# Applying the second model's first norm factor to the products' results

## The chip, the cores and the metric

The kernel runs on one NeuronCore of a Trainium2 chip (trn2). The metric is the time of one execution on the device in microseconds (us); lower is better. The core has five engines that run their own instruction streams in order and meet at semaphores: TensorE (PE in the rows, its weight load PEld), VectorE (DVE), ScalarE (ACT), GpSimd (POOL), and SyncE (SP), which here only issues transfers. All arithmetic is float32; a float32 matrix product is made of three float32r products.

## The reference

Two models run one after the other on 256 tokens of 1024 features. The first ends in a feed-forward layer and a layer norm, the second begins with an RMS norm and one wide input product. Cut to what lies on both sides of the boundary:

```python
x = layer_norm(ALPHA * x + swiglu_ffn(x, ffn_w_in[i], ffn_w_down[i]), ln_ffn_g[i], ln_ffn_b[i])
...
h = rmsnorm(x, ln1[l])                    # x * rsqrt(mean(x * x) + 1e-6) * g
z = h @ w_in[l]
ml_qk, ml_v, ml_o, ml_i, ml_f, fx_q, fx_k, fx_v, fx_f = jnp.split(z, splits, axis=-1)
ml_qk = jax.nn.silu(causal_conv(ml_qk, ml_conv_w[l], ml_conv_b[l]))
...
x = x + cross_attention(rmsnorm(x, ln_x[l]), rmsnorm(mem, ln_mem[l]), w_xq[l], w_xkv[l], w_xo[l])
```

ml_i, ml_f and fx_f are the gates (16 columns); the mLSTM takes ml_qk, ml_v, ml_o, the forgetting attention fx_q, fx_k, fx_v.

## The kernel before

Tokens lie in two tiles of 128 rows (TT = 2), features in eight tiles of 128 (KT = 8). `x_tm` holds the residual token-major, `x_hi` and `x_lo` the normalized rows feature-major, split into a float32r high part and the rest. All big weights come as 164 slabs of 128x2048, streamed in order by SyncE through three raw buffers. For each slab ScalarE makes `w_hi` (line 602), VectorE `w_lo = w_raw - w_hi` (line 1364), each in a ring of three (WS = 3), and TensorE forms hi x hi, lo x hi and hi x lo (lines 2087 to 2089). `after(i)` on ScalarE and VectorE is the split of slab i + 3; ScalarE's waits until TensorE is done with slab i, VectorE's until ScalarE is, and SyncE's load of slab i + 3 until VectorE is done with slab i. The order on each engine is written out by hand.

The input product of the second model takes 14 slabs: ml_qk 4, ml_v 2, ml_o 2, fx_qk 4, fx_v 2. ml_qk and fx_qk come out feature-major (features on partitions), ml_v, ml_o and fx_v token-major. Each goes to one of three PSUM banks and ScalarE takes it from there (`take`, line 1061); TensorE's slab n waits for take n - 3. Behind the first ml_qk slab TensorE does the gate product (`gates`, 24 matmuls).

Norms are numbered. Norm 3 is the first model's last layer norm, norm 4 the second model's first RMS norm, norm 5 that of `mem`. A usual layer norm (`norm`, lines 981 and 1683, used for norms 0 to 2) takes statistics on VectorE, the root on ScalarE, writes normalized rows to `xn`, and lets TensorE transpose them (`transposes`, line 2490), with `warm` matmuls of the identity (line 2158) between; gain and offset are applied per feature behind the transposes, and POOL makes x_tm from xn with `gain_offset` (lines 1328 and 1329), spread over the next feed-forward layer. Norms 3 and 4 together are `last_of_first_model` (lines 1000 and 1713): VectorE applies norm 3's gain and offset to x_tm by rows, ScalarE squares the rows (line 913), takes the roots, and only then are the rows of norm 4 normalized and transposed.

After that ScalarE starts the transfer of `mem` into `gain` (line 1142); VectorE makes the gates' logarithms, running sums and maxima (lines 1905 to 1913) with ScalarE's Exp and Ln between, then four w_lo, the memory norm, and the convolution over ml_qk (lines 1928 and 1936). POOL has nothing to do in the second model.

Of the kernel before, what the change touches and what calls it, by code (L numbers as in the profile page):

```python
# [157 lines left out]
def build(nc, d, out, upto=99):  # L158
# [4 lines left out]
    with ExitStack() as ctx:  # L163
# [107 lines left out]
        gsel = sb("gsel", [P, 12, P], F32R, a_m)  # L271
        sel = sb("sel", [P, 12], where=a_m)
# [21 lines left out]
        with ExitStack() as a:  # L294
# [15 lines left out]
            se_o = sb("se_o", [P, 2, T], where=a)  # L310
            ml_y = x_fm[:, 0:4, :].rearrange("p a (b c) -> p (a b) c", c=P)
# [144 lines left out]
        rstd_ready, xn0_ready, xn_act, xn_dve = sem("rstd_ready"), sem("xn0_ready"), sem("xn_act"), sem("xn_dve")  # L456
        zero_set, half_hi = sem("zero_set"), sem("half_hi")
# [9 lines left out]
        STATS_BEFORE = {0: 0, 1: 2, 2: 4, 3: 6, 4: 8, 8: 11}  # L467
# [118 lines left out]
        def _(act):  # L586
# [354 lines left out]
            def to_features(q, k):  # L941
# [39 lines left out]
            def norm(q, second=None):  # L981

                if NORMS[q][4]:
                    for t in range(TT):
                        deviation(q, t)
                        normalized(q, t, x_tm)
                        if t == 0:
                            hi_half(second, 0)
                else:
# [10 lines left out]
            def last_of_first_model():  # L1000
# [145 lines left out]

            def takes(section, n, dst, scale=lambda j: 1.0):
                for j in range(n):
                    take(P_FIRST[section] + j, first[section] + j, dst(j), scale(j))
            takes("ml_qk", 4, lambda j: conv_in[:, 2 * j:2 * j + 2, 3:T + 3])  # L1150
# [3 lines left out]
            act.wait_ge(mem_loaded, 16)  # L1154
            for t in range(TT):
                squares_of_all(5, t, gain)
            normalized(5, 1, gain)
            takes("ml_v", 2, lambda j: ml_v[:, :, 256 * j:256 * j + 256])
# [5 lines left out]
            for j in range(2):  # L1164
                act.wait_ge(slab_done, first["ml_o"] + j + 1)
                n = P_FIRST["ml_o"] + j
                nc.scalar.activation(ml_o[:, :, 256 * j:256 * j + 256], ps[:, n % 3, :].rearrange("p (a b) -> p a b", a=2),
                                     ACT.Sigmoid).then_inc(p_taken, 1)
                after(first["ml_o"] + j)
# [4 lines left out]
            dst = lambda j: fx_v[:, :, 256 * j:256 * j + 256]  # L1174
            take(P_FIRST["fx_v"], first["fx_v"], dst(0))
# [4 lines left out]
            take(P_FIRST["fx_v"] + 1, first["fx_v"] + 1, dst(1))  # L1180
# [83 lines left out]
        def _(pool):  # L1264
# [68 lines left out]
            for q in range(3):  # L1333
                pool.wait_ge(xlo_ready, KT * FM_NORMS.index(q) + KT)
                pool.wait_ge(gain_loaded, 32 * (q + 1))
                for t in range(TT):
                    for n in range(2):
# [4 lines left out]
                        gain_offset(q, t, n)  # L1342


        @block.vector
        def _(dve):
# [274 lines left out]
            def scales(q, t):  # L1621
# [3 lines left out]
                if NORMS[q][4] and q != 3:  # L1625
# [14 lines left out]
            def to_features(q, k):  # L1640

                name, g_at, b_at, e, mean = NORMS[q]
                dve.wait_ge(tr_ready, KT * FM_NORMS.index(q) + 2 * (k // 2) + 2)
                if b_at:
# [38 lines left out]
            def norm(q, scale, last_slab, product):  # L1683
# [9 lines left out]
                features(q)  # L1693
# [18 lines left out]

            def last_of_first_model(scale, last_slab, product):

                def centred(t, at):
                    return V.scalar_tensor_tensor(x_tm[:, t, at], x_tm[:, t, at], mv[:, t, 0:1], gain[:, 0, at],
                                                  ALU.subtract, ALU.mult)

                def scaled(t, at):
                    dve.wait_ge(rstd_ready, 6 + t + 1)  # L1720
                    V.scalar_tensor_tensor(x_tm[:, t, at], x_tm[:, t, at], rstd[:, t:t + 1], gain[:, 1, at],
                                           ALU.mult, ALU.add).then_inc(stat_ready, 1)

                first_half_sums(scale, last_slab, product)
                dve.wait_ge(gain_loaded, 128)
                link(centred(0, slice(0, C)))
                scales(3, 0)
                link(add_product(x_tm, scale, 1, 1, last_slab, product))
                link(half_statistics(1, 1))
                mean_variance(1)  # L1730
                scaled(0, slice(0, C))
                scales(3, 1)
                link(centred(1, slice(0, 512)))
                scaled(1, slice(0, 512))
                link(centred(1, slice(512, C)))
# [150 lines left out]
            for i in (2, 3):  # L1886
                after(first["moba_o"] + i)
# [1009 lines left out]
```

## Time and profile before

| | us |
|---|---|
| median of 3 runs (1186.64 to 1189.3) | 1189.04 |
| the profiled execution | 1189.56 |
| its span, first to last instruction | 1187.8 |
| TensorE busy | 1147.4 |
| VectorE busy | 746.9 |
| ScalarE busy | 621.1 |
| POOL busy | 109.9 |

All rows of this document are of one profiled execution; their times count from the span's start. Engines overlap, so busy times don't add up. The chain that ended last is the sequence of instructions that released one another up to the end; its shares say where a saved microsecond would count. A duration includes the time that an instruction waits for a port after its issue. TensorE's matmuls are pipelined: a record is longer than the distance to the next one, and the distance is what counts. The mean granted clock of TensorE was 0.997 of full speed.

### The profile page before, as it was taken

The numbers are of one execution on the slowest core, as the hardware profiler recorded it, in microseconds if no ns is written. First come the engines' busy times: TensorE is split into PE (matmuls) and PEld (weight loads), VectorE is DVE, ScalarE is ACT, GpSimd is POOL, SyncE is SP. The second block draws the span as 40 slices with busy tenths as digits, with TensorE's granted clock in tenths as the row PEclk, the third lists the DMA queues.
The fourth block names the chain that finished last, engine by engine and source line by source line (L and its number), as shares of the span: only waits on it lengthen the run. The fifth ranks groups of instructions, "written<-read, shape, count | busy, mean of one in ns | idle before, by whom it ended". The sixth has DMA issues, their size and how long they took to land.

```text
span 1187.8 us, 24912 instructions
## 1 busy us (share of the span) xinstructions
PE 1147.4 (97%) x10626; PEld 1046.4 (88%) x10626; DVE 746.9 (63%) x1081; ACT 621.1 (52%) x906; POOL 109.9 (9%) x87
## 2 busy tenths in 40 slices
PE   6999989999999999999999999999998999999997
PEld 6798777789999989987999999899997898999996
DVE  7888776475544467896655444768486555655554
ACT  8974553354344345664733433665565564544443
POOL 0032263601100000220010000000000000000000
PEclk9999999999999999999999999999999999999999
DMA  8531111046545644433555446354533442655550
GB/s 302 217 106 50 50 49 49 25 156 231 190 167 188 246 179 156 165 109 141 178 213 182 179 172 248 107 211 177 179 118 131 143 176 92 239 180 181 212 177 36
DMA packets 29805, 187.32 MB, mean 158 GB/s; under 512 B 3472, under 2 KB 5648, under 8 KB 8592
## 3 DMA queue, kind: packets, MB, share of 16 engines
q1 hardware_dynamic: 27072, 177.21, 41.4%
q10 hardware_dynamic: 2640, 8.75, 2.3%
q8 instruction: 73, 1.20, 0.4%
q14 instruction: 20, 0.16, 0.0%
HBM read 184.90 MB, written 1.05 MB: 157 GB/s over the span
## 4 chain that ended last, share of the span: by engine, by line
PE 82%; DVE 10%; ACT 4%; issue 2%; DMA 0%; POOL 0%; ACTq 0%; DVEq 0%; SPq 0%
PE ps L2087 24%; PE ps L2088 23%; PE ps L2089 23%; DVE w_lo L1364 1%; PE ps L2411 1%; PE ps L2416 1%; PE ps L2557 1%; PE ps L2220 1%; ACT mixed L631 1%; DVE w_lo L1360 1%; PE ps L2413 1%; PE ps L2304 1%; PE ps L2353 1%; PE ps L2799 1%; PE ps L2807 1%
## 5 line engine op out<-in xcount | busy, mean ns | idle before, releaser
L1364 DVE TENSOR_TENSOR w_lo<-w_raw,w_hi 128x2048 fp32r<-128x2048 f32 x149 | 346.0, 2339 | 133.2 <-ACT w_hi L602 132.8
L2087 PE MATMUL ps<-x_hi,w_hi 128*128 128x256 f32 x1344 | 378.2, 281 | 4.3 <-DVE x_lo L1651 2.4
L2088 PE MATMUL ps<-x_lo,w_hi 128*128 128x256 f32 x1344 | 374.9, 279 | 0.0
L2089 PE MATMUL ps<-x_hi,w_lo 128*128 128x256 f32 x1344 | 374.8, 279 | 0.0
L602 ACT CAST w_hi<-w_raw 128x2048 fp32r<-128x2048 f32 x148 | 281.7, 1906 | 150.2 <-PE ps L2089 149.1
L2087 PEld LDWEIGHTS ps<-x_hi,w_hi 128*128 128x128 f32 x1344 | 252.6, 188 | 10.7 <-issue 5.6
L2088 PEld LDWEIGHTS ps<-x_lo,w_hi 128*128 128x128 f32 x1344 | 252.7, 188 | 1.3
L2089 PEld LDWEIGHTS ps<-x_hi,w_lo 128*128 128x128 f32 x1344 | 252.7, 188 | 0.0
L2087 PE MATMUL ps<-w_hi,hid_hi 128*128 128x512 f32 x304 | 118.7, 391 | 0.1
L2088 PE MATMUL ps<-w_lo,hid_hi 128*128 128x512 f32 x304 | 118.7, 390 | 0.0
L2089 PE MATMUL ps<-w_hi,hid_lo 128*128 128x512 f32 x304 | 118.3, 389 | 0.0
L1779 DVE TENSOR_TENSOR hid<-act_f,ps 128x512 f32<-128x512 f32 x22 | 15.1, 688 | 127.0 <-PE ps L2089 127.0
L1033 ACT ACTIVATE act_f<-ps 128x512 f32<-128x512 f32 x38 | 22.7, 598 | 123.4 <-PE ps L2089 123.4
L2087 PE MATMUL ps<-w_hi,mix_hi 128*128 128x512 f32 (+1 forms) x192 | 73.0, 380 | 0.6 <-DVE mix_lo L1829 0.3
L2088 PE MATMUL ps<-w_lo,mix_hi 128*128 128x512 f32 (+1 forms) x192 | 68.1, 354 | 0.0
L2089 PE MATMUL ps<-w_hi,mix_lo 128*128 128x512 f32 (+1 forms) x192 | 68.0, 354 | 0.0
L2089 PEld LDWEIGHTS ps<-w_hi,hid_lo 128*128 128x128 f32 x304 | 57.1, 188 | 12.2
L2087 PEld LDWEIGHTS ps<-w_hi,hid_hi 128*128 128x128 f32 x304 | 57.1, 188 | 11.4 <-DVE hid_lo L1785 0.5
L2088 PEld LDWEIGHTS ps<-w_lo,hid_hi 128*128 128x128 f32 x304 | 57.1, 188 | 10.5
L2087 PE MATMUL ps<-w_hi,x_hi 128*128 128x256 f32 x224 | 63.0, 281 | 0.0
L2089 PE MATMUL ps<-w_hi,x_lo 128*128 128x256 f32 x224 | 62.9, 281 | 0.0
L2088 PE MATMUL ps<-w_lo,x_hi 128*128 128x256 f32 x224 | 62.9, 281 | 0.0
(399 smaller groups left out, 1779.0 us busy)
## 6 DMA issues: line engine op xcount, KB each, us to landing
w_raw<-in_weights SPq DMA_DIRECT2D x163, 1024.0 KB, 4.9
xt<-in_xT SPq DMA_DIRECT2D x2, 512.0 KB, 5.4
w_raw<-in_weights SPq DMA_DIRECT2D x2, 512.0 KB, 6.2
x_tm<-in_x SPq DMA_DIRECT2D x1, 1024.0 KB, 5.0
gain<-in_mix_g ACTq DMA_DIRECT2D x2, 512.0 KB, 3.7
gain<-in_mix_b ACTq DMA_DIRECT2D x2, 512.0 KB, 5.9
gain<-in_ffn_g ACTq DMA_DIRECT2D x2, 512.0 KB, 7.4
gain<-in_ffn_b ACTq DMA_DIRECT2D x2, 512.0 KB, 9.5
```

The lines of the kernel that those rows point to most:

```text
L602: nc.scalar.copy(w_hi[:, i % WS, :], w_raw[:, i % RAW, :]).then_inc(hi_done, 1)
L631: nc.scalar.activation(mixed[:, q % 2, k, :], xt[:, k, :], ACT.Copy, scale=less_mu[:, at:at + 1]).then_inc(scaled_ready, 1)
L1033: nc.scalar.activation(act_f[:, j % 2, :], ps[:, 4 + 2 * (j % 2), :], ACT.Relu if name == "ff2" else ACT.Silu).then_inc(ffn_act, 1)
L1360: ins = V.tensor_tensor(halves_placed(w_lo[:, i % WS, :], m), halves_first(w_raw[:, i % RAW, :], m), halves_placed(w_hi[:, i % WS, :], m). ...
L1364: V.tensor_tensor(w_lo[:, i % WS, :], w_raw[:, i % RAW, :], w_hi[:, i % WS, :].bitcast(F32), ALU.subtract).then_inc(lo_done, 1)
L1779: V.tensor_tensor(hid[:, j % 2, :], act_f[:, j % 2, :], ps[:, 5 + 2 * (j % 2), :], ALU.mult).then_inc(ffn_taken, 1)
L2087: nc.tensor.matmul(out, hi_l, hi_r, start=start, stop=False)
L2088: nc.tensor.matmul(out, hi_l, lo_r, start=False, stop=False)
L2089: return nc.tensor.matmul(out, lo_l, hi_r, start=False, stop=stop)
L2220: last = mm(both[q][:, T * m + c0:T * m + T], src[f, 2 * m + t, :], ar[f, 2 * g + m, t, :, :].rearrange("p s c -> p (s c)")[:, c0:T], star ...
L2304: last = mm(z[half, HD * h:HD * h + HD], dd[half, t, 0, s, :], u_m[half, HD * h:HD * h + HD], start=True, stop=True)
L2353: last = mm(ps[0:hi_c - lo_c, 5, at:at + T], g1[:, k, lo_c:hi_c], mixed[:, 1, k, :], start=k == 0, stop=k == KT - 1)
```

## The change

Norm 3 becomes a usual norm. Its normalized rows are transposed, and behind the transposes each feature is multiplied by norm 3's gain times norm 4's, plus norm 3's offset times norm 4's (two small tiles computed earlier). What remains of norm 4 is one factor per token, which commutes with the product. It is formed while the products run: POOL makes x_tm (8 instructions), ScalarE squares it, VectorE inverts the root (`factor_col`), spreads it over 128 columns (`factor_wide`), TensorE transposes it behind the third ml_qk slab, and VectorE copies it out (`factor_row`). Token-major results are scaled in ScalarE's take (one instruction per row tile in place of one), the gates by VectorE, feature-major ones by eight multiplies of POOL; the convolution waits for four of them, the mLSTM's scores for all. The gate chain moves behind this and behind the memory norm; `mem` goes to conv_out's space.

```diff
@@ ScalarE, features @@
+                if q == 4:
+                    return nc.scalar.activation(x_fm[:, k, :], feature_tile(q, k), ACT.Identity,
+                                                scale=ln1_gain[:, k:k + 1], bias=ln1_offset[:, k:k + 1])
@@ ScalarE @@
+            def squares_of_residual():
+                junk = x_fm[:, :, :].rearrange("p (t a) c -> p t (a c)", t=TT)
                 for t in range(TT):
-                    deviation(3, t)
-                act.wait_ge(stat_ready, STATS_BEFORE[4] + 1)
-                squares_of_all(4, 0, x_tm)
-                squares_of_half(4, 0)
-                normalized(4, 0, x_tm)
-                squares_of_half(4, 1)
-                normalized(4, 1, x_tm)
-                features(4)
+                    act.wait_ge(xtm_ready, 7 + t)
+                    link(nc.scalar.activation(junk[:, t], x_tm[:, t, :], ACT.Square, accum_out=square[:, t:t + 1]))
+                    nc.scalar.activation(factor_dev[:, t:t + 1], square[:, t:t + 1], ACT.Sqrt, scale=1.0 / C,
+                                         bias=eps_c[:, 2:3]).then_inc(sd_ready, 1)
...
-            last_of_first_model()
-            for i in (31, 32):
-                after(first["ffn1"] + i)
-            nc.scalar.dma_start(gain[:, :, :], d["mem"]).then_inc(mem_loaded, 16)
+            norm(3, first["ffn1"] + 31 + WS)
+            nc.scalar.dma_start(mem_tm, d["mem"]).then_inc(mem_loaded, 16)
...
+            def take_scaled(name, j, dst, func=ACT.Copy):
+                n = P_FIRST[name] + j
+                act.wait_ge(slab_done, first[name] + j + 1)
+                for t in range(TT):
+                    ins = nc.scalar.activation(dst[:, t, 256 * j:256 * j + 256], ps[:, n % 3, T * t:T * t + T], func,
+                                               scale=factor_col[:, t:t + 1])
+                ins.then_inc(p_taken, 1)
+                after(first[name] + j)
+            takes("ml_qk", 4, conv_part, js=(0, 1))
+            squares_of_residual()
+            act.wait_ge(mem_loaded, 16)
+            for t in range(TT):
+                squares_of_all(5, t, mem_tm)
+            takes("ml_qk", 4, conv_part, js=(2,))
+            normalized(5, 1, mem_tm)
             act.wait_ge(gate_abs, 1)
             link(nc.scalar.activation(za[:, :], za[:, :], ACT.Exp, scale=-1.0))
             nc.scalar.activation(za[:, :], za[:, :], ACT.Ln, bias=1.0).then_inc(gate_ln, 1)
+            takes("ml_qk", 4, conv_part, js=(3,))
@@ POOL, at its end @@
+            pool.wait_ge(xlo_ready, KT * FM_NORMS.index(4) + KT)
+            pool.wait_ge(gain_loaded, 128)
+            for t in range(TT):
+                for n in range(2):
+                    gain_offset(3, t, n)
+            pool.wait_ge(factor_set, 1)
+            for name, n in (("ml_qk", 4), ("fx_qk", 4)):
+                for j in range(n):
+                    pool.wait_ge(p_taken, P_FIRST[name] + j + 1)
...
+                    nc.gpsimd.tensor_tensor(part, part, over(factor_row, 2), ALU.mult).then_inc(factored, 1)
@@ VectorE, behind norm 3 @@
+            for j in range(2):
+                after(first["ml_qk"] + j)
+            for t in range(TT):
+                dve.wait_ge(sd_ready, 8 + t + 1)
+                ins = V.reciprocal(factor_col[:, t:t + 1], factor_dev[:, t:t + 1])
+                ins.then_inc(rstd_ready, 1)
+            dve.wait_ge(rstd_ready, 10)
+            V.tensor_scalar(factor_wide, along(factor_col[:, :], P), 1.0, None, ALU.mult).then_inc(factor_spread, 1)
+            dve.wait_ge(mem_loaded, 16)
+            scales(5, 0)
+            normalized(5, 0, slice(0, C), mem_tm)
+            scales(5, 1)
+            normalized(5, 1, slice(0, 512), mem_tm)
+            dve.wait_ge(factor_tr, 1)
+            link(V.tensor_scalar(factor_row, ps[:, 5, 0:T], 1.0, None, ALU.mult))
             dve.wait_ge(gate_mm, 1)
...
+            V.tensor_tensor(ml_z, ps[0:36, 3, 0:T], factor_row[0:36], ALU.mult).then_inc(factor_set, 1)
...
-            for j in range(4):
+            for j in range(2, 4):
                 after(first["ml_qk"] + j)
...
-            dve.wait_ge(p_taken, P_FIRST["ml_qk"] + 4)
+            dve.wait_ge(factored, 4)
+            dve.wait_ge(xn_act, FM_NORMS.index(5) + 1)
@@ TensorE @@
-            pe.wait_ge(stat_ready, STATS_BEFORE[3] + 1)
-            transposes(4, ((1, 30), (0, 0), (0, 0)))
+            transposes(4, ((0, 0), (1, 7), (1, 4)))
...
+                    if name == "ml_qk" and j == 2:
+                        pe.wait_ge(factor_spread, 1)
+                        for t in range(TT):
+                            last = nc.tensor.transpose(ps[:, 5, P * t:P * t + P], factor_wide[:, t, :], ident)
+                        last.then_inc(factor_tr, 1)
...
             pe.wait_ge(silu_ready, 2)
+            pe.wait_ge(factored, 8)
```

## Rows read from the trace of the kernel before

**Rows 1.** The page, parts 1 and 4: TensorE's busy time, chain that ended last.

```profile
PE 1147.4 (97%) x10626; PEld 1046.4 (88%) x10626; DVE 746.9 (63%) x1081; ACT 621.1 (52%) x906; POOL 109.9 (9%) x87
...
PE 82%; DVE 10%; ACT 4%; issue 2%; DMA 0%; POOL 0%; ACTq 0%; DVEq 0%; SPq 0%
```

**Rows 2.** Timeline, TensorE, boundary: start us, us, engine, line, operation, count.

```profile
752.19 0.39 PE L2089 MATMUL ps<-w_hi,hid_lo 128*128 128x512 f32 x1
752.42 6.86 PE L2158 MATMUL ps<-base_c 128*128 128x128 f32 x60
...
763.41 0.36 PE L2087 MATMUL ps<-x_hi,w_hi 128*128 128x256 f32 x1 [0.90 <-DVE x_lo L1651]
```

**Rows 3.** Timeline, TensorE: last product and first matmul at norms 1 and 2.

```profile
443.61 0.39 PE L2089 MATMUL ps<-w_hi,hid_lo 128*128 128x512 f32 x1
...
449.13 0.36 PE L2087 MATMUL ps<-x_hi,w_hi 128*128 128x256 f32 x1
...
561.59 0.39 PE L2089 MATMUL ps<-w_hi,mix_lo 128*128 128x512 f32 x1
...
567.85 0.36 PE L2087 MATMUL ps<-x_hi,w_hi 128*128 128x256 f32 x1 [0.55 <-DVE x_lo L1651]
```

**Rows 4.** Timeline, VectorE, at the boundary, idle time and its releaser in brackets.

```profile
760.68 0.16 DVE L1624 RECIPROCAL rstd<-sd 128x1 f32<-128x1 f32 x1 [2.22 <-ACT sd L924]
```

**Rows 5.** Timeline, VectorE: the last two x_lo at norm 1.

```profile
451.88 1.48 DVE L1651 TENSOR_TENSOR x_lo<-x_fm,x_hi 128x512 fp32r<-128x512 f32 x2
```

**Rows 6.** Timeline, POOL and VectorE: one alone, then both at the same time.

```profile
277.77 1.30 POOL L1328 TENSOR_TENSOR x_tm<-xn,gain 128x512 f32<-128x512 f32 x1 [42.35 <-DVE hid_lo L1785]
...
518.36 3.22 POOL L1329 TENSOR_TENSOR x_tm<-x_tm,gain 128x512 f32<-128x512 f32 x1
...
517.99 2.45 DVE L1364 TENSOR_TENSOR w_lo<-w_raw,w_hi 128x2048 fp32r<-128x2048 f32 x1 [2.19 <-ACT w_hi L602]
520.36 1.77 DVE L1829 TENSOR_TENSOR mix_lo<-ma_o,mix_hi 128x512 fp32r<-128x512 f32 x1
```

**Rows 7.** Timeline, ScalarE, from the gates to the second ml_v slab.

```profile
775.50 1.28 ACT L1145 ACT_TABLE_LOAD   x1
776.80 0.42 ACT L1145 ACTIVATE za<-za 12x256 f32<-12x256 f32 x1
...
783.80 0.60 ACT L1061 ACTIVATE xk_fm<-ps 128x512 f32<-128x512 f32 x1 [2.03 <-PE ps L2089]
784.29 1.90 ACT L602 CAST w_hi<-w_raw 128x2048 fp32r<-128x2048 f32 x1
789.40 0.60 ACT L1061 ACTIVATE xk_fm<-ps 128x512 f32<-128x512 f32 x1 [3.21 <-PE ps L2089]
...
794.97 1.04 ACT L913 ACTIVATE xn<-gain 128x1024 f32<-128x1024 f32 x1
...
796.13 0.29 ACT L914 ACTIVATE sd<-square,eps_c 128x1 f32<-128x1 f32 x1
796.66 0.72 ACT L938 ACTIVATE xn<-gain,rstd 128x512 f32<-128x512 f32 x1 [0.23 <-DVE rstd L1624]
...
800.77 0.60 ACT L1061 ACTIVATE ml_v<-ps 128x512 f32<-128x512 f32 x1 [1.10 <-PE ps L2089]
```

**Rows 8.** Timeline, VectorE: the gate chain's second part, and two w_lo behind it.

```profile
777.25 0.28 DVE L1909 TENSOR_SCALAR zf<-zf 12x256 f32<-12x256 f32 x1 [2.21 <-ACT za L1145]
...
779.88 4.50 DVE L1364 TENSOR_TENSOR w_lo<-w_raw,w_hi 128x2048 fp32r<-128x2048 f32 x2
```

**Rows 9.** Stretches: length, busy PE, PEld, DVE, ACT, POOL (instructions), granted clock, DMA share, GB/s.

```profile
145.00:150.00 5.00, 4.19 (x119) 3.55 (x116) 3.97 (x10) 1.99 (x6) 1.48 (x2) 0.94 0.19 52
150.00:155.00 5.00, 4.85 (x159) 4.35 (x156) 3.14 (x7) 1.88 (x4) 4.03 (x6) 0.72 0.00 0
...
1180.00:1181.00 1.00, 0.77 (x4) 0.31 (x2) 0.69 (x2) 0.00 (x0) 0.00 (x0) 1.00 0.00 0
...
1183.00:1184.00 1.00, 0.00 (x0) 0.00 (x0) 1.00 (x2) 0.00 (x0) 0.00 (x0) 0.81 0.00 0
```

More of the change, by code:

```diff
@@ L271, in build @@
         gsel = sb("gsel", [P, 12, P], F32R, a_m)
+        ln1_gain, ln1_offset = (sb(n, [P, KT], where=a_m) for n in ("ln1_gain", "ln1_offset"))
         sel = sb("sel", [P, 12], where=a_m)
@@ L310, in build @@
             se_o = sb("se_o", [P, 2, T], where=a)
+            factor_col, factor_dev = (sb(n, [P, TT], where=a) for n in ("factor_col", "factor_dev"))
+            factor_wide = se_s[:, 0, 0:T].rearrange("p (t c) -> p t c", t=TT)
+            factor_row = se_s[:, 1, 0:T]
+            mem_tm = conv_out[:, :, :].rearrange("p (t a) c -> p t (a c)", t=TT)
+            ml_z = fx_q[0:36, 0, :]
             ml_y = x_fm[:, 0:4, :].rearrange("p a (b c) -> p (a b) c", c=P)
@@ L456, in build @@
         rstd_ready, xn0_ready, xn_act, xn_dve = sem("rstd_ready"), sem("xn0_ready"), sem("xn_act"), sem("xn_dve")
+        factor_spread, factor_tr, factor_set, factored = (
+            sem(n) for n in ("factor_spread", "factor_tr", "factor_set", "factored"))
         zero_set, half_hi = sem("zero_set"), sem("half_hi")
@@ L1137, in _, with takes @@
             ffn("ffn1")
-            last_of_first_model()
-            for i in (31, 32):
-                after(first["ffn1"] + i)
-            nc.scalar.dma_start(gain[:, :, :], d["mem"]).then_inc(mem_loaded, 16)
+            norm(3, first["ffn1"] + 31 + WS)
+            nc.scalar.dma_start(mem_tm, d["mem"]).then_inc(mem_loaded, 16)
+            def takes(section, n, dst, scale=lambda j: 1.0, js=None):
+                for j in js or range(n):
+                    take(P_FIRST[section] + j, first[section] + j, dst(j), scale(j))
+            def take_scaled(name, j, dst, func=ACT.Copy):
[6 more added lines that the diff above has]
+                after(first[name] + j)
+            conv_part = lambda j: conv_in[:, 2 * j:2 * j + 2, 3:T + 3]
+            takes("ml_qk", 4, conv_part, js=(0, 1))
[5 more added lines that the diff above has]
+            normalized(5, 1, mem_tm)
             act.wait_ge(gate_abs, 1)
@@ L1145, in _ @@
             nc.scalar.activation(za[:, :], za[:, :], ACT.Ln, bias=1.0).then_inc(gate_ln, 1)
[L1147 to L1150, printed above, removed]
+            takes("ml_qk", 4, conv_part, js=(3,))
             act.wait_ge(gate_rows, 1)
@@ L1153, in _ @@
             nc.scalar.copy(gi_s[0:4], gi[0:4, :]).then_inc(row_hi, 1)
[L1154 to L1158, printed above, removed]
+            for j in range(2):
+                take_scaled("ml_v", j, ml_v)
             for k in (0, 1, 6, 7):
@@ L1164, in _ @@
             for j in range(2):
[L1165 to L1169, printed above, removed]
+                take_scaled("ml_o", j, ml_o, ACT.Sigmoid)
             act.wait_ge(conv_ready, 1)
@@ L1173, in _ @@
                   lambda j: (HD ** -0.5, 1.0)[j // 2])
-            dst = lambda j: fx_v[:, :, 256 * j:256 * j + 256]
-            take(P_FIRST["fx_v"], first["fx_v"], dst(0))
+            take_scaled("fx_v", 0, fx_v)
             act.wait_ge(slab_done, first["fx_v"] + 2)
@@ L1179, in _ @@
                 high_part(2 * i, 2)
-            take(P_FIRST["fx_v"] + 1, first["fx_v"] + 1, dst(1))
+            take_scaled("fx_v", 1, fx_v)
             def take_memory(n):
@@ L1624, in scales @@
                 ins = V.reciprocal(rstd[:, t:t + 1], sd[:, t:t + 1])
-                if NORMS[q][4] and q != 3:
+                if NORMS[q][4]:
                     link(ins)
@@ L1643, in to_features @@
                 dve.wait_ge(tr_ready, KT * FM_NORMS.index(q) + 2 * (k // 2) + 2)
+                if q == 4:
+                    return V.tensor_scalar(x_fm[:, k, :], feature_tile(q, k), ln1_gain[:, k:k + 1], ln1_offset[:, k:k + 1],
+                                           ALU.mult, ALU.add)
                 if b_at:
@@ L1711, in sums_and_features @@
                 lo_half(1).then_inc(lo_done, 1)
[L1713 to L1735, printed above, removed]
-                scaled(1, slice(512, C))
-                scales(4, 0)
-                scales(4, 1)
-                normalized(4, 1, slice(0, 512), x_tm)
-                features(4)
             def last_norm(last_slab, product):
@@ L1887, in _ @@
                 after(first["moba_o"] + i)
+            for dst, name in ((ln1_gain, "ln_ffn_g"), (ln1_offset, "ln_ffn_b")):
+                V.tensor_tensor(dst[:, :], par[:, PCOL[name] + KT:PCOL[name] + 2 * KT], par[:, PCOL["ln1_2"]:PCOL["ln1_2"] + KT],
+                                ALU.mult)
             V.tensor_tensor(sel[:, :], ident[:, 0:12], ident[:, 32:RS], ALU.add).then_inc(sel_set, 1)
@@ L1894, in _ @@
             dve.wait_ge(xtm_ready, 6)
-            last_of_first_model(ALPHA, first["ffn1"] + 32, 4)
+            norm(3, ALPHA, first["ffn1"] + 32, 4)
             for i in (31, 32):
```

21 lines of the change are left out of this document (11 added, 10 removed).

## The prediction

> **What bounds the kernel now.** I read the page first: TensorE is busy for 97% of the span and holds 82% of the chain that ended last [rows 1]. Time can be won only where TensorE waits or does filler work, and is lost wherever a new wait stops it. Then the timeline of TensorE at the boundary between the models. The last product of the first model starts at 752.19 us and the first matmul of the second model's first product, which I call Q0, at 763.41: 11.22 us. Most of it is filler (60 records of the warming matmuls of line 2158, 6.86 us) and two sets of transposes that wait for normalized rows [rows 2]. The reader should see the same stretch at two other layer norms: 443.61 to 449.13 is 5.52 us and 561.59 to 567.85 is 6.26 us [rows 3]. The excess at this boundary is the second norm's work, which ends in VectorE's wait of 2.22 us for the root of the RMS norm [rows 4]. After Q0 TensorE never waits until the last of the input products: 14 slabs follow one another at 5.6 to 5.7 us each [rows 7]. What keeps it fed is the split of each slab, ScalarE's w_hi and then VectorE's w_lo, three slabs ahead.
>
> **Part 1, the boundary: a gain.** The change makes this norm the same code as the norm of rows 3 (one norm, rows normalized by ScalarE and VectorE, transposes with 7 and 4 warming matmuls behind them). Two precomputed columns take the place of the parameters, at the same instruction count. So the stretch falls from 11.22 to 5.52 us: -5.70 us; by the other norm it would be -4.96. I take the first, because the work ahead of it (w_lo, four sums, statistics) is the same; its warming counts are the same too. Q0 then starts at 752.19 + 5.52 = 757.7. All times below are those of the profiled run, with the change's own waits worked out on top; what happens unhindered is 5.7 us earlier than before.
>
> **Part 2, TensorE's added work.** Two transposes of the spread factor. The 60 filler records took 6.86 us, 0.114 each [rows 2]; two transposes are 2 to 4 such records, 0.23 to 0.46 us. I take 0.3. Nothing hides them.
>
> **Part 3, the factor's way, and POOL.** The factor needs x_tm, the first model's result, so gain and offset of norm 3, until now on VectorE inside the boundary, move to POOL: two row tiles x two halves x two instructions, 8 in all, each undisturbed 1.30 us [rows 6]. They start when the last x_lo is written. At the twin norm that ends at 451.88 + 1.48 = 453.36 [rows 5], 9.75 us behind the last product, so here at 761.9. Alone, 8 x 1.29 = 10.3 us would end at 772.3. But just then VectorE makes w_lo of the next slabs. Rows 6 show what happens: while VectorE's w_lo runs from 517.99 to 520.44, POOL's multiply issued at 518.36 takes 3.22 us instead of 1.3; it runs after it, not beside it. VectorE's next subtraction, issued at 520.36, takes 1.77 us and ends at 522.13, after POOL's end at 521.58: it waits too. They take strict turns. Four w_lo fall into POOL's stretch (two ordered behind the norm, then two for the slabs that Q0 and Q1 free), at 2.25 us each [rows 8]: 9.0 us. POOL ends at 762.0 + 10.3 + 9.0 = 781.3.
> The Trainium skill, page "SBUF — State Buffer", section "Who interferes with whom", says the same of a VectorE instruction with two SBUF inputs against a GpSimd instruction that reads SBUF, and its section "A bandwidth-pool intuition that's wrong" adds about 115 ns for the blocked one at each hand-over. The row shows none of that: 518.36 + 3.22 - 1.30 = 520.28, no later than VectorE's end. By the page's figure some eight turns would add 0.9 us, an estimate from that page; the sum goes by the row.
>
> **Part 4, the first new wait.** ScalarE squares row tile 1 only then: square and root of a 1024-wide row took 794.97 to 796.42, 1.45 us [rows 7]; so 782.75. VectorE's reciprocal, 0.16 [rows 4], and the spread over 128 columns, which I put at 0.5 for 256 columns (w_lo of 2048 columns takes 2.25), end at 783.4. TensorE's in-order stream has the transposes of that tile behind Q2. Before, ScalarE took Q2 at 783.80 after waiting for TensorE [rows 7]; 5.7 earlier is 778.0. So TensorE stands still 5.4 us, then transposes, and starts Q3 at 783.7, where it was before. The boundary's gain is spent here. Queued behind TensorE's wait is everything; behind ScalarE's wait for POOL are the memory's squares, the take of Q2, w_hi of slab +5 and the gates' Exp.
>
> **Part 5, the second new wait.** VectorE's stream now has the memory norm and the gate chain ahead of the w_lo of slab V1 (the second ml_v slab), where before the gate chain came right behind gates. ScalarE from 782.75: the memory's two squares 2.8, take and w_hi of Q2 2.35, its half of the memory norm 0.65, a table load 1.28 (788.5 to 789.8), Exp when VectorE's |z| is there (about 790.4, since POOL's multiplies by the factor hold VectorE up), 0.42, a table load 1.28, Ln 0.42 [rows 7]: 792.5. VectorE's five instructions from there to the next w_lo took 777.25 to 779.88, 2.63 us [rows 8]; one of them meets POOL's fourth multiply, released by the take of Q3 at 793: +1.2. Then 2.29 for w_lo: 798.6. TensorE has Q3 and V0 until 783.7 + 5.6 + 5.7 = 795.0 and waits 3.6 us for it. Before, V1 began at 800.77 - 5.7 = 795.0 as well. From there every engine keeps its phase: convolution, gate rows and w_lo follow the same distance behind, and POOL's four multiplies of fx_qk lie in idle time of VectorE.
>
> **Part 6.** The takes of token-major products become two instructions; only the last one, ahead of the memory's first product, lies in TensorE's way: +0.25 (two of some 0.42 for one of 0.6). The mem transfer moves from gain to conv_out and is issued at about 764, 18 us ahead of its use at 782.75: nothing.
>
> **Sum.** -5.70 + 5.4 + 0.3 + 3.6 + 0.25 = +3.85 us. Profiled run 1189.56 (span 1187.8 and 1.8 around it) gives 1193.4; the median of the three runs is 0.5 lower, so 1192.9.
>
> **Rivals.** A measurement here tells about 0.3%, 3.6 us, from no change.
> (a) No turns: POOL works beside VectorE, or nearly. Against it is every meeting in rows 6; for it only that the twin norm's own POOL work lay elsewhere, so no row shows eight in a run. It decides if POOL is done before w_hi of the slab behind Q1 ends on ScalarE (774.7). Then the factor is spread at 778.3, TensorE waits 0.3, and w_lo of V1, at 791.7 by the same chain less POOL, costs 1.5: -5.7 + 0.3 + 0.3 + 1.5 + 0.25 = -3.35, 1185.7. Chance 0.13, faster or within 0.3% in equal parts.
> (b) The first wait comes, the second doesn't: Exp's table is loaded ahead or POOL's multiplies miss the gate chain, and the slack hides the rest. -5.7 + 5.7 + 0 to 1.5 = about +1, 1189.5 to 1190.5. Chance 0.17, same.
> (c) Forecast: 0.58. With the part 1 saving between 4.96 and 5.70 and POOL's time between 9.8 and 11 us it lies between +2.5 and +5.5; half of it is beyond 0.3%.
> (d) The clock joins in. At the kernel's end TensorE's last matmul lies in 1180 to 1181 and the granted clock was 0.81 in 1183 to 1184, half after it; at 145 to 155 it was 0.94 and 0.72 over two stretches of 5 us, which is 0.34 x 5 = 1.7 us of full clock lost [rows 9]. A first wait of 5.4 us is long enough for that drop (to 1.2 of 2.4 GHz). I cost it at nothing, because Q3 and V0 then run into the second wait and only shorten it. If it isn't absorbed, or comes at the second wait: +1.7 and up, 1194.6 to 1198. The Trainium skill, "TensorE: Matmul & The Clock Gate", section "Why this matters for your kernels", asks to leave no idle gaps between bursts for this reason; the trace agrees. Chance 0.12.
>
> **How the numbers follow.** Slower by over 0.3%: half of (c) and all of (d), 0.29 + 0.12 = 0.41, raised to 0.44 since several small terms (hand-overs, two-instruction takes) only add. Faster: 0.07. Same: the rest, 0.49. Range: from 1187.5, which leaves out (a), to 1197.0, which takes in most of (d).
>
> **What would show it.** Right: POOL's first eight instructions at 762 to 781 with durations of 1.3 and 3.4 to 3.6 us mixed; TensorE idle about 5 us ahead of the transposes of factor_wide and about 3.5 ahead of V1; Q0's first matmul 5.5 us behind the last product; convolution 3 to 4 us later than 797.96. Wrong: POOL finished by 773, a wait at the factor below 1 us, or w_lo of V1 ready before V0 ends.

## The result, and the profile after

The change made the kernel slower: 1197.72 us (1196.19 to 1200.48) against 1189.17 us (1186.64 to 1190.57) of the kernel before beside it, ratio 1.0071 with a 95% interval of 1.0058 to 1.0083, which is +8.5 us (6.9 to 9.9). The forecast was +3.85 us, with a range that ended at 1197.0, and it held "the same" (0.49) a little likelier than "slower" (0.44). The profiled execution took 1196.3 us, its span 1194.4. First the page of the changed kernel, TensorE's busy time and the chain that ended last, against [rows 1]:

```profile
PE 1148.9 (96%) x10590; PEld 1042.9 (87%) x10590; DVE 749.9 (63%) x1082; ACT 621.3 (52%) x909; POOL 137.7 (12%) x103
...
PE 81%; DVE 10%; ACT 4%; POOL 2%; issue 2%; DMA 1%; ACTq 0%; SPq 0%; DVEq 0%; POOLq 0%
```

TensorE is busy for 1.5 us more with 36 instructions less, POOL has come into the chain. The timeline of TensorE in the changed kernel, at the boundary, at the factor's transposes and at V1 (V0 and V1 are the two ml_v slabs, Q0 to Q3 the four ml_qk slabs; start, us, engine, line, operation; idle time and releaser in brackets):

```profile
753.21 0.39 PE L2110 MATMUL ps<-w_hi,hid_lo 128*128 128x512 f32 x1
...
758.74 0.35 PE L2108 MATMUL ps<-x_hi,w_hi 128*128 128x256 f32 x1
...
783.60 0.69 PE L2709 MATMUL ps<-base_c,se_s 128*128 128x128 f32 x2 [4.17 <-DVE se_s L1920]
...
799.36 0.36 PE L2108 MATMUL ps<-w_hi,x_hi 128*128 128x256 f32 x1 [1.31 <-DVE w_lo L1396]
```

From the last product to Q0 it is 5.53 us, against 11.22 in [rows 2]. Both new waits are there. The last product lies 1.02 us later than before, so 783.60 and 799.36 are 782.6 and 798.3 by the clock of the forecast. POOL's timeline (first three and last of the eight instructions of norm 3):

```profile
763.04 1.30 POOL L1345 TENSOR_TENSOR x_tm<-xn,gain 128x512 f32<-128x512 f32 x1 [129.47 <-DVE x_lo L1686]
764.42 3.23 POOL L1346 TENSOR_TENSOR x_tm<-x_tm,gain 128x512 f32<-128x512 f32 x1
767.61 3.34 POOL L1345 TENSOR_TENSOR x_tm<-xn,gain 128x512 f32<-128x512 f32 x1
...
780.25 1.26 POOL L1346 TENSOR_TENSOR x_tm<-x_tm,gain 128x512 f32<-128x512 f32 x1
```

18.5 us for eight instructions, four of them stretched to 3.2 to 3.3 us. And the granted clock of TensorE over stretches of 2 us (length, busy, clock, DMA share, GB/s):

```profile
780.00:782.00 2.00, 0.00 (x0) 1.00 0.83 250
782.00:784.00 2.00, 0.40 (x3) 0.70 0.65 274
784.00:786.00 2.00, 2.00 (x11) 0.50 0.03 8
786.00:788.00 2.00, 2.00 (x11) 0.50 0.00 0
788.00:790.00 2.00, 2.00 (x13) 0.59 0.00 0
```

In the 4.2 us of idleness the clock falls to its lower level (1.2 GHz), and it is there while Q3 runs: 0.6 + 1.0 + 1.0 + 0.8 = 3.4 us of full clock are lost.

**What is not at the boundary.** ScalarE's instructions lie 0.74 us later than before just ahead of the boundary (750 us) and 4.56 us later behind it (826 us). Of these 3.8 us the boundary section has 3.5 to 3.6 (0.28 is the last slab ahead of it), so the forecast's +3.85 holds within 0.4 us. The rest is spread over the three feed-forward layers: there the distance between the traces grows by 0.12 us with every down-product slab (24 matmuls), though not one instruction of them was changed. The groups of instructions show it, with their shapes kept apart (count, busy us, mean ns). Before, then after:

```profile
L2087 PE MATMUL ps<-w_hi,hid_hi 128*128 128x512 f32 x304 | 118.7, 391 | 0.1
```

```profile
L2108 PE MATMUL ps<-w_hi,hid_hi 128*128 128x512 f32 x304 | 120.2, 395 | 0.1
```

What counts is the distance from one such matmul to the next. The first and the last of the 24 matmuls of one slab, 23 distances apart, before and then after:

```profile
1025.42 0.39 PE L2087 MATMUL ps<-w_hi,hid_hi 128*128 128x512 f32 x1
...
1030.66 0.39 PE L2089 MATMUL ps<-w_hi,hid_lo 128*128 128x512 f32 x1
```

```profile
1030.38 0.39 PE L2108 MATMUL ps<-w_hi,hid_hi 128*128 128x512 f32 x1
...
1035.74 0.39 PE L2110 MATMUL ps<-w_hi,hid_lo 128*128 128x512 f32 x1
```

That is 5.24 and 5.36 us. The mean distance over all slabs is 0.2276 us before and 0.2330 after, and nearly the same in each, those in loops and those outside. There are three such groups of 304, so 912 x 0.0054 = 4.9 us. What the change did to them is to move them: `ln1_gain` and `ln1_offset` are 64 bytes per partition, allocated ahead of `hid_hi` and `hid_lo`, which the matmuls load as their stationary operand.

### The profile page after: what moved, and what is told of

The parts are those of the page before. It is cut to its first block, busy times and chain, and to the rows that moved or that the text cites. A ratio compares the mean times of both kernels' runs of the same rounds, so it can differ in the third digit from the quotient of the medians.

```text
span 1194.4 us, 24862 instructions
## 1 busy us (share of the span) xinstructions
PE 1148.9 (96%) x10590; PEld 1042.9 (87%) x10590; DVE 749.9 (63%) x1082; ACT 621.3 (52%) x909; POOL 137.7 (12%) x103
## 4 chain that ended last, share of the span: by engine, by line
PE 81%; DVE 10%; ACT 4%; POOL 2%; issue 2%; DMA 1%; ACTq 0%; SPq 0%; DVEq 0%; POOLq 0%
PE ps L2108 24%; PE ps L2110 23%; PE ps L2109 23%; DVE w_lo L1396 1%; PE ps L2437 1%; POOL x_tm L1345 1%; POOL x_tm L1346 1%; PE ps L2578 1%; PE ps L2432 1%; PE ps L2325 1%; PE ps L2241 1%; PE ps L2374 1%; PE ps L2825 1%; PE ps L2833 1%; PE ps L2301 1%
## 5 line engine op out<-in xcount | busy, mean ns | idle before, releaser
L1345 POOL TENSOR_TENSOR x_tm<-xn,gain 128x512 f32<-128x512 f32 x16 | 26.2, 1637 | 492.9 <-PE ps L2615 185.5
```

The lines of the kernel that those rows point to most:

```text
L1345: plink(nc.gpsimd.tensor_tensor(x_tm[:, t, at], xn[:, t, at], gain[:, 0, at], ALU.mult))
```

## The experiments

**e1, the displacement alone.**

```diff
         gsel = sb("gsel", [P, 12, P], F32R, a_m)
+        spare = sb("spare", [P, 16], where=a_m)
```

> The kernel before with one unused tile of 64 bytes per partition right behind gsel, so that hid_hi and hid_lo (and all that lies behind them) start 64 bytes later, as in the changed kernel; no instruction is added or changed. In the changed kernel the 912 matmuls of the down products with hid_hi or hid_lo as stationary operand stand 0.2330 us apart in place of 0.2276 us. Placement theory: that comes from where the stationary operand starts in SBUF, so here too 0.2330 us and 912 x 0.0054 = 4.9 us more than before (+0.41%). Rival: it comes from the changed instruction streams or from the run; then the spacing stays at 0.2276 us and the time within 0.5 us of before.

Measured: 1194.01 us against 1189.04, ratio 1.0041 (1.0028 to 1.0054), +5.0 us. Spacing 0.2332 us; the group in e1:

```profile
L2088 PE MATMUL ps<-w_hi,hid_hi 128*128 128x512 f32 x304 | 120.2, 395 | 0.1
```

Sixty-four unused bytes cost 5 us. This is shown, not argued: nothing else differs. The placement theory held.

**e2, the change without the displacement.**

```diff
-        ln1_gain, ln1_offset = (sb(n, [P, KT], where=a_m) for n in ("ln1_gain", "ln1_offset"))
+        ln1_gain, ln1_offset = par[:, 0:KT], par[:, KT:2 * KT]
```

> The changed kernel with ln1_gain and ln1_offset put into sixteen columns of par that nothing reads any more (rwkv_mu), so that every tile lies where it lay before. Placement theory: spacing of the down products back at 0.2276 us, 4.9 us less than the changed kernel, so before + 3.5 to 4 us (+0.31%), which is the boundary section alone, forecast at +3.85. Rival (streams or chance): the same +8.5 us (+0.71%) as the changed kernel.

Measured: 1193.83 us, ratio 1.0039 (1.0026 to 1.0052), +4.6 us (3.1 to 6.2). Spacing 0.2278. The displacement is out, and what remains is the boundary section; the forecast's +3.85 lies in its interval, the changed kernel's +8.5 does not. TensorE's waits from 770 to 860 us in e2 (total us, times, longest):

```profile
PE ps L2709 <- DVE se_s L1920: 4.2, 1, 4.2
PE ps L2108 <- DVE w_lo L1396: 1.8, 1, 1.8
```

**e3, another displacement of the kernel before.**

```diff
+        spare_x = sb("spare_x", [P, 24], where=a_m)
         x_hi = sb("x_hi", [P, KT, T], F32R, a_m)
...
         gsel = sb("gsel", [P, 12, P], F32R, a_m)
+        spare = sb("spare", [P, 8], where=a_m)
```

> The kernel before with 96 unused bytes ahead of x_hi and 32 behind gsel: x_hi, x_lo, xn, x_fm, gain and xk_fm, which start 32 bytes beyond a multiple of 128, now start on one, and hid_hi and hid_lo stay on one (moved by 128). Nothing else changes. If any start off a multiple of 128 costs a stationary operand some 0.005 us a matmul, the 672 matmuls with x as stationary operand get 3.6 us cheaper: before - 3.6 us (-0.30%). If an offset of 32 bytes costs nothing, or only the step of 64 matters: within 0.6 us of before. The down products should stay at 0.2276 us either way, which tests that a move by 128 bytes is harmless.

Measured: 1200.86 us, ratio 1.0100 (1.0086 to 1.0115), +11.8 us. Both readings fell: a start on a multiple of 128 is not what matters, and 128 bytes are as bad for hid as 64. The groups in e3:

```profile
L2089 PE MATMUL ps<-x_hi,w_hi 128*128 128x256 f32 x1344 | 382.3, 284 | 4.1 <-DVE x_lo L1653 2.4 <-DVE x_lo L1662 0.5 <-DVE w_lo L1362 0.3
...
L2089 PE MATMUL ps<-w_hi,hid_hi 128*128 128x512 f32 x304 | 120.0, 395 | 0.1
```

Within the steady slabs x as moving operand went from 0.1167 to 0.1186 us (0.1199 in the first feed-forward layer), and the down products from 0.2276 to 0.2323. With the means over the whole trace this is 4032 x 0.0022 + 912 x 0.0045 = 13 us, close to what was measured.

**e5, TensorE alone.** No diff: a kernel of matmuls only, blocks with one displacement each.

> A kernel of matmuls alone, which computes nothing of the reference: w_hi and w_lo lie at the addresses of the kernel before, one tile st starts where hid_hi started (a multiple of 1024 bytes beyond w_hi), and TensorE runs the same triples back to back. (i) down product, hi part at st + off, lo part 4096 bytes further, off from 0 to 992 in steps of 32 bytes, 24 matmuls of 512 columns each; (ii) the same with off 0 and w moved by 0 to 960 bytes in steps of 64; (iii) x as the moving operand of 256 columns at st + off, lo 8192 bytes further, 48 matmuls each; (iv) x as the stationary operand, the same. Placement theory: the spacing is a function of the distance between the two operands' starts; (i) gives 0.227 us at off 0 and 0.233 at 64 and 128, (ii) moves in the same way with w, (iii) gives 0.1167 at off 288 (as in the kernel before) and some 0.119 at 384. Rival: placement matters only through what other engines read and write at the same time; then, with no other engine at work, all of (i) and (ii) are equal within 0.0005 us.

The fourth and the last matmul of four blocks, from TensorE's timeline in e5: the down product at 0 and at 64 bytes, then x moving at 32 and at 192:

```profile
39.84 0.39 PE L199 MATMUL ps<-w_hi,st 128*128 128x512 f32 x1
...
44.38 0.39 PE L201 MATMUL ps<-w_hi,st 128*128 128x512 f32 x1
...
51.64 0.39 PE L199 MATMUL ps<-w_hi,st 128*128 128x512 f32 x1
...
56.30 0.39 PE L201 MATMUL ps<-w_hi,st 128*128 128x512 f32 x1
...
330.10 0.28 PE L199 MATMUL ps<-st,w_hi 128*128 128x256 f32 x1
...
335.24 0.27 PE L201 MATMUL ps<-st,w_lo 128*128 128x256 f32 x1
...
360.27 0.28 PE L199 MATMUL ps<-st,w_hi 128*128 128x256 f32 x1
...
365.27 0.28 PE L201 MATMUL ps<-st,w_lo 128*128 128x256 f32 x1
```

Twenty distances in the first two pairs, 44 in the others: 0.2270, 0.2330, 0.1168 and 0.1136 us. All blocks together, worked out in the same way, repeat with a period of 256 bytes, nearly all to within 0.0005 us (hid at 0 to within 0.001: 4.54 to 4.56 us for twenty distances):

| bytes beyond a multiple of 256 | 0 | 32 | 64 | 96 | 128 | 160 | 192 | 224 |
|---|---|---|---|---|---|---|---|---|
| hid stationary, 512 columns | 0.2270 | 0.2335 | 0.2330 | 0.2340 | 0.2325 | 0.2335 | 0.2295 | 0.2330 |
| x moving, 256 columns | 0.1200 | 0.1168 | 0.1177 | 0.1200 | 0.1189 | 0.1173 | 0.1136 | 0.1182 |
| x stationary, 256 columns | 0.1198 | 0.1182 | 0.1134 | 0.1186 | 0.1184 | 0.1198 | 0.1177 | 0.1166 |

Moving w in place of hid by 0, 64, 128, 192 gives 0.2275, 0.2285, 0.2320, 0.2335, again with the period of 256. These are the values of hid at 0, 192, 128 and 64 to within 0.001 us: moving w forwards does what moving hid back does, so it is the distance between the two that counts. The two rows of x say the same: x stationary at d bytes takes what x moving takes at 256 - d, in seven of eight phases to within 0.0005 us (at 96 it is 0.1186 against 0.1173). No other engine works in e5, so it is no contention with one; the rival fell. The table gives the steady values of the kernels so far to within 0.0003 us, or 0.0006 for hid at 0: before (hid 0, x 32), after and e1 (hid 64), e3 (hid 128, x 128). It does not give the 0.1199 of e3's first feed-forward layer. The Trainium skill, page "SBUF — State Buffer", section "Operand start alignment", asks only for a start at a multiple of the element size, 4 bytes here, and says that this is about legality and that its runs timed nothing; these runs add what the start costs in time.

**e8, the best place for x, on the kernel before.**

```diff
+        spare_x = sb("spare_x", [P, 40], where=a_m)
         x_hi = sb("x_hi", [P, KT, T], F32R, a_m)
...
         gsel = sb("gsel", [P, 12, P], F32R, a_m)
+        spare = sb("spare", [P, 24], where=a_m)
```

> The kernel before with 160 unused bytes per partition ahead of x_hi and 96 behind gsel: x_hi and x_lo start 192 bytes (not 32) beyond a multiple of 256 from w_hi, hid_hi and hid_lo stay at 0 (moved by 256). In e5 the spacing with x as moving operand is 0.1168 us at 32 and 0.1136 us at 192, and has a period of 256 bytes. Placement theory: 4032 matmuls x 0.0032 = 12.9 us less and 672 with x stationary x 0.0005 = 0.3 less: before - 10 to - 13 us (-0.84 to -1.1%), down products unchanged at 0.2276. Rival: what e5 shows for TensorE alone is hidden in the kernel by the splits of ScalarE and VectorE or the transfers (5.6 us a slab), and the time stays within 3 us of before.

Measured: 1188.66 us, ratio 0.9993 (0.9981 to 1.0004). The time is the rival's, but for another reason than it gives. Two stretches of TensorE's timeline in e8, 57 distances in a projection and 45 in a feed-forward slab:

```profile
774.77 0.28 PE L2089 MATMUL ps<-x_hi,w_hi 128*128 128x256 f32 x1
...
781.23 0.28 PE L2089 MATMUL ps<-x_hi,w_hi 128*128 128x256 f32 x1
...
1039.90 0.28 PE L2091 MATMUL ps<-x_hi,w_lo 128*128 128x256 f32 x1
...
1045.20 0.28 PE L2091 MATMUL ps<-x_hi,w_lo 128*128 128x256 f32 x1
```

0.1133 us in the first, near the table's 0.1136, and 0.1178 in the second and in all feed-forward layers, without a wait in either. Most projection slabs run at the lower value, but not all: the first two fx_qk slabs, at 811 to 822 us, take 0.1178 as well. So one placement can run at two rates, as in e3, and the table is not all of it. The move by 256 bytes of hid was harmless (0.2269), as the period asks.

**e9, hi and lo parts moved apart.**

> As e5 (matmuls alone, nothing of the reference), 24 matmuls a block, period of 256 taken as given: x moving with the starts of x_hi and x_lo varied independently over eight phases of 32 bytes; the down product with those of hid_hi and hid_lo; x moving with x and w_lo; x stationary with x_hi and x_lo. If each matmul's spacing depends on its own two operands (the stationary tile being loaded and the moving tile being read), the spacing of a block is a sum of terms, one for each pair, and the best combination has both at their best phase, 0.1136 us or a little below. If TensorE's read streams share one pattern, other combinations come out far better, towards 0.107 us, the time of 256 columns at 2.4 GHz.

Neither held. 192 of the 256 blocks have 256 columns and took 0.1134 to 0.1210 us, far from 0.107; for x moving the best was 0.1140, with x and w_lo moved. With both parts of x moved alike, six of the eight phases gave what e5 gives (0.1195 at 0), but 192 gave 0.1175 in place of 0.1136, and 160 gave 0.1185 in place of 0.1173; the lo part lies 8448 bytes behind the hi part here in place of 8192, and blocks are half as long. What picks the rate stays open.

**e6, POOL's part cut short.** On e2:

```diff
-                at = slice(512 * n, 512 * n + 512)
+                at = slice(512 * n, 512 * n + (32 if q == 3 else 512))
```

> e2 with POOL's eight gain_offset(3) instructions cut from 512 to 32 columns each (x_tm beyond them stays without norm 3's gain and offset, so this part of the computation is left out): POOL is done at about 763 and no longer alternates with VectorE. If POOL's time of 18.5 us is what makes the first wait, TensorE's wait at the factor falls from 4.2 us to below 1 us, the clock does not fall at 779 to 787 (3.4 us of full clock in e2), and the time is that of the forecast's case without turns: before - 3.4 us (e2 - 7 to - 8 us). Rival: ScalarE's order (squares behind the takes of Q0 and Q1) or the second wait holds the end anyway: the first wait goes but the one ahead of V1 grows from 1.8 to 5 us or more, and the time is before + 0 to + 2 us.

Measured: 1192.26 us, ratio 1.0023 (1.0013 to 1.0032), +2.7 us. TensorE's waits from 770 to 860 us in e6, and the clock around the second:

```profile
PE ps L2108 <- DVE w_lo L1396: 4.1, 1, 4.1
...
PE ps L2709 <- DVE se_s L1920: 0.2, 1, 0.2
```

```profile
790.00:792.00 2.00, 0.00 (x0) 0.95 0.00 0
792.00:794.00 2.00, 0.49 (x2) 0.50 0.00 0
```

The first wait went from 4.2 to 0.2 us, so POOL made it. But the one ahead of V1 grew from 1.8 to 4.1, and now the clock fell in that one (it is low from 791.8 to 798.6), where nothing absorbs it: V1 takes 8.0 us in place of 5.7. Boundary, Q0 to Q2, transposes, first wait, second wait, V1 and take: -5.7 + 0.4 + 0.3 + 0.2 + 4.1 + 2.3 + 0.25 = +1.85, inside the interval (+1.5 to +3.8). The expectation's rival is what came: the second wait is the one that decides.

**e7, TensorE kept busy in the first wait.** On e2:

```diff
+                        warm(ps[:, 5, :], 32)
                         pe.wait_ge(factor_spread, 1)
```

> e2 with 32 warming matmuls (128 columns, 3.6 us) ahead of TensorE's wait for the spread factor, so that it is busy through most of the 4.2 us. The granted clock should then stay at its upper level through 779 to 787. If the lost clock lies in Q3 and V0 and only shortens the wait ahead of V1, as the forecast costed it, that wait grows from 1.8 to some 4 to 5 us and the time equals e2's within 0.5 us. Rival (the clock joins in): e2 - 1.5 to - 3.4 us.

Measured: 1194.10 us, ratio 1.0036 (1.0024 to 1.0049): e2's time. Each of the 32 took 0.228 us (two records), so the filler lasted 7.3 us, not 3.6, and ran 3 us past the factor. Even so TensorE's wait ahead of V1 is 1.8 us, as in e2:

```profile
PE ps L2108 <- DVE w_lo L1396: 1.8, 1, 1.8
```

```profile
782.00:784.00 2.00, 2.00 (x20) 1.00 0.00 0
784.00:786.00 2.00, 2.00 (x20) 1.00 0.00 0
```

The clock stayed at its upper level (2.4 GHz), and what that saved went into the filler; V1 started when its w_lo was there. So the clock lost at the first wait costs nothing at the end, as the forecast had it, and neither do 3 us of useless work.

**e4, the order mended.** On e2: the factor's transposes behind Q3, Q2's take ahead of the squares, the w_lo of V1 ahead of the gate chain.

```diff
@@ TensorE @@
-                    if name == "ml_qk" and j == 2:
+                    if name == "ml_qk" and j == 3:
@@ ScalarE @@
-            takes("ml_qk", 4, conv_part, js=(0, 1))
+            takes("ml_qk", 4, conv_part, js=(0, 1, 2))
             squares_of_residual()
...
+            take_scaled("ml_v", 0, ml_v)
             act.wait_ge(gate_rows, 1)
@@ VectorE, behind the spread factor @@
+            after(first["ml_qk"] + 2)
             dve.wait_ge(factor_tr, 1)
...
+            scales(5, 0)
+            normalized(5, 0, slice(0, C), mem_tm)
+            scales(5, 1)
+            normalized(5, 1, slice(0, 512), mem_tm)
+            after(first["ml_qk"] + 3)
             dve.wait_ge(gate_ln, 1)
...
+            after(first["ml_v"])
             dve.wait_ge(row_hi, 1)
```

> e2 with the order around the factor mended: TensorE transposes the factor behind Q3 and not behind Q2; ScalarE takes Q2 before the squares of x_tm and V0 before the gate rows; VectorE makes the w_lo of V1 right behind the spread factor, the memory norm and the w_lo of the first ml_o slab inside the gates' wait for Exp and Ln, the w_lo of the second ml_o slab ahead of the convolution. By my account both new waits of TensorE (4.2 us at the factor, 1.3 us ahead of V1, and the lower clock between them) come from order alone, so they vanish: -5.7 + 0.3 + 0.25 = -5.1 us, before - 5.1 us (-0.43%). Rival: POOL's eight and four instructions slow VectorE so much that its w_lo become the limit in any order; then a wait of 2 to 4 us turns up ahead of the ml_o slabs and the time is before - 1 to + 1 us.

Measured: 1187.37 us, ratio 0.9989 (0.9980 to 0.9999), -1.3 us. The forecast for this run, -5.1, was missed. Both waits are gone, but two others have come (1.4 and 0.3 us); TensorE's waits from 770 to 930 us in e4:

```profile
PE ps L2695 <- DVE bias L1980: 2.2, 1, 2.2
PE ps L2695 <- DVE bias L1978: 1.4, 1, 1.4
...
PE ps L2105 <- ACT fx_v L1159: 0.4, 1, 0.4
PE ps L2675 <- DVE gst L1940: 0.3, 1, 0.3
```

The 2.2 us are there in the kernel before too, but in e4's trace the clock falls behind them (897 to 901, 1.7 us) and in that of before not. -5.1 + 1.4 + 0.3 + 1.7 = -1.7. The rival, VectorE as the limit, had a part, 1.4 us, and its -1 to +1 us is nearer to what was measured.

**e10, e11, e12, towards a better kernel.** e10 is e4 with the placement of e8 and this on VectorE (the two to_features lines come back behind the second bias row; factor_col and factor_dev, which is not shown, move into the unused bytes behind gsel):

```diff
-            for i in (1, 2):
-                to_features(5, 2 * i)
-                to_features(5, 2 * i + 1).then_inc(xfm_ready, 1)
             dve.wait_ge(gate_cols, 1)
...
+            rows(0, 0)
             after(first["ml_o"] + 1)
```

> e4 (the change with its order mended) with the placement of e8, and on VectorE the first bias row ahead of a w_lo and the memory's x_fm behind the second bias row, for the wait of 1.4 us that e4 shows ahead of the second gate row. Sum: e4's gain of 1.7 us (its own measurement) + 1.4 for the wait + 12.9 for the placement: before - 14 to - 16 us (-1.2 to -1.35%). Rival: faster slabs make VectorE the limit in the mLSTM section, where it has 2.3 us of w_lo and the convolution against shorter slabs; then new waits of 1 to 3 us ahead of the ml_o and fx_qk slabs and before - 11 to - 13 us.

Measured: 1186.99 us, ratio 0.9971 (0.9958 to 0.9985), -3.4 us. The forecast was missed by over 10 us. The wait of 1.4 us is gone; the placement, as in e8, brought little of the 12.9 us: Q1 to Q3, at 0.1135 us a matmul in e8, run at 0.1178 here. The clock behind the wait of 2.2 us, in e10:

```profile
892.00:894.00 2.00, 0.01 (x1) 1.00 0.59 250
894.00:896.00 2.00, 2.00 (x9) 0.52 0.00 0
```

e11 takes that wait away:

```diff
-            out_low(O_FX, se_o, slice(4, 6))
             rows(1, 9)
+            out_low(O_FX, se_o, slice(4, 6))
```

> e10 with one exchange on VectorE: the bias row of row product 9 comes ahead of the mix_lo that waits for ScalarE (VectorE is idle for 3.6 us there), so TensorE finds it taken when it comes to row product 10. In e10 TensorE waits 2.2 us for it and the granted clock falls right behind (894 to 898, 1.7 us of full clock), as it does in e2, e4, e6, e7 and e8, but not in the traces of before and after. If both go: e10 - 2.2 - 1.7 = e10 - 3.9 us (before - 6 to - 7 us, -0.55%). Rival: only the wait goes and comes back at the scores behind it (0.5 us there now), the clock falls elsewhere: e10 - 0 to - 1.5 us.

Measured: 1182.12 us, ratio 0.9933 (0.9917 to 0.9949), -8.0 us, which is 4.6 below e10 (3.9 were forecast). The largest wait from 770 to 930 us in e11 is

```profile
PE ps L2578 <- DVE se_s L1831: 0.7, 1, 0.7
```

and the clock stays up until the kernel's end. e12 is e11 without the unused bytes:

> e11 without the unused bytes, so every tile lies where it lay in the kernel before (x_hi at 32 in the period of 256 bytes, hid_hi at 0). In e8 the move of x_hi from 32 to 192 gave 0.1134 us in most projection slabs but 0.1178 in the feed-forward layers (0.1167 before in both), which adds up to nothing: so e12 equals e11 within 1.5 us, and e12 against before is the change plus its mended order alone, before - 5 to - 7 us. Rival: the placement of x is worth something in the combined kernel (e10 shows 0.1176 as its mean against 0.1179 in e4, 4032 matmuls, 1.2 us), and e12 is 1.5 to 3 us slower than e11.

Measured: 1183.15 us, ratio 0.9938 (0.9924 to 0.9952), -7.4 us: the two agree within their intervals, and the placement of x is worth nothing that can be told here. Not all of the 7.4 us is the change's: the wait of 2.2 us that e11 takes away is in the kernel before too, and the kernel before with that one exchange was not run, so how much of the gain it would have without the change is open.

## Why the prediction was wrong

**The boundary section was right in its sum.** Point by point, from the traces of after, e2, e6 and e7:

| term | forecast | measured |
|---|---|---|
| boundary (part 1) | -5.70 | 5.53 in place of 11.22: -5.69 |
| Q0 to Q2 | nothing | +0.4 |
| two transposes (part 2) | +0.3 | 0.5, at the lower clock |
| POOL's eight instructions (part 3) | 19.3 us | 18.5 us |
| first wait (part 4) | 5.4 | 4.2 |
| clock behind it (rival d) | nothing | Q3 and V0 14.0 in place of 11.3: +2.7 |
| second wait (part 5) | 3.6 | 1.3 (1.8 in e2) |
| last take (part 6) | +0.25 | 0.4 in place of 0.2: +0.2 |
| sum (POOL's row is inside the first wait) | +3.85 | +3.6; e2: +4.6 (3.1 to 6.2) |

The first wait is 1.2 us shorter because POOL is done 0.8 us earlier and Q2 ends 0.4 us later than I put it. The clock fell in it, which made Q3 and V0 2.7 us longer, and the second wait is 2.3 us shorter. V1 starts when its w_lo is ready: 798.3 by the forecast's clock against 798.6. e7 shows directly that the time between the waits doesn't count. What I costed at nothing, the clock at the first wait, did cost nothing, under the condition that I gave; e6 shows the other case of rival (d), a fall in the last wait, which cost V1 2.3 us.

**The step that failed was one that isn't in the sum.** Part 1 says of the two small tiles that "two precomputed columns take the place of the parameters, at the same instruction count": they were costed as instructions, and not as 64 bytes ahead of `hid_hi` and `hid_lo`. The allocation is the line that e2 takes away, and the order of allocation in the kernel shows what lies behind it. I took it that a matmul lasts the same wherever its operands lie. The term that the sum lacks is this one: e1 puts it at +5.0 us with nothing else changed, e2 takes it out again. From the traces 3.6 + 4.9 = 8.5, as measured. That it comes out to a tenth is luck: the interval is 6.9 to 9.9, e2 and e1 by their medians add up to 9.6, and three of the changed kernel's six executions, those from 1198.5 us up, had a mean granted clock of 0.993 in place of 0.995 to 0.996. The two profiled executions differ by 6.7 only: the trace of before lost 1.7 us of clock at 149 to 153 us [rows 9], that of after did not.

**The rivals.** (a) had the wrong mechanism: POOL and VectorE took turns as [rows 6] had it, and even without these turns (e6) the time was not 1185.7, since the second wait was 4.1 us and not 1.5. My account of (a) took out all of POOL's turns, but its first three multiplies by the factor still meet three instructions of the gate chain ahead of Exp (1.28, 1.27 and 1.20 us in e6). The first of them in the changed kernel, where the instruction ahead of it, of the same width, took 0.42 us:

```profile
787.29 1.28 DVE L1931 TENSOR_SCALAR zf<-fx_q,gate_bf 12x256 f32<-12x256 f32 x1
```

(b), the second wait hidden, did not occur in this order of work; e4 shows that order is what makes both waits, and that VectorE's load then makes one of 1.4 us elsewhere. (d) is right about the fall and right that it is absorbed here.

## What to carry to other kernels

A tile added anywhere in a list of allocations moves all behind it. Compare the addresses of the operands of the commonest matmul before and after a change, keep their distance to each other (modulo 256 bytes in these runs), and put a new small tile at the end or into spent columns. Don't expect a gain from looking for a better place: one that is best in a kernel of matmuls alone (e5) brought nothing that can be told in the whole kernel (e8). When a trace drifts away steadily through code that wasn't touched, take the group of instructions whose mean changed by a per cent: 0.005 us in 912 matmuls was more than the whole boundary. A first wait that runs into a second one is not worth mending; look for the last wait, and for what is late there.

## What the runs showed of the hardware

- The time from one float32r matmul to the next depends on how far apart their two operands start, with a period of 256 bytes: 0.2270 to 0.2340 us for 512 columns and 0.1134 to 0.1200 for 256, with no other engine at work (e5). In whole kernels that was +5.0 us for 64 bytes (e1) and +11.8 us for 96 and 128 (e3).
- With x at 192 bytes the same code ran at 0.1133 us in most projection slabs and at 0.1178 in feed-forward layers (e8), with x at 128 at 0.1186 and 0.1199 (e3). Why was not found.
- Behind idle stretches of 4.2 us (after, e2) and 4.1 us (e6) the granted clock fell to its lower level, 3.4 us of full clock each, of which 2.2 to 2.7 fell on matmuls. Behind the wait of 2.2 us near 898 us it fell in the traces of e2, e4, e6, e7, e8 and e10, 1.7 us each, and did not in those of before, after, e1 and e3. What tells these apart is not known, but taking the wait away (e11) gave 4.6 us where the wait alone is 2.2.
- The clock also fell near 149 us (before, e1, e7, e8, e12) or near 180 us (e4, e10, e12), 1.7 us each time, and in neither place in after, e2, e3, e6 and e11. None of the edits changes an instruction there. So the traces of two kernels can differ by 1.7 us or more for no reason that lies in the change; medians, or stretches with the clock beside them, are what to compare.
